# Three norms of a streaming encoder step: other homes for early split weights, four output tiles per row, and the rows' sum one chunk later

## The chip, the core and the metric

The kernel runs on one core of a Trainium2 chip. The metric is the device time of one execution in microseconds (us). Before the change it is 2686.58 us, the median of three runs (2686.34 to 2686.86). PE is TensorE's matmul stream, PEld its weight loads, DVE is VectorE, ACT ScalarE, POOL GpSimd, SP SyncE.

## What is computed

One inference step of a two-layer trunk on 288 tokens (256 of a new stream, 32 of a running one), model width 2048. Layer 0 mixes with a gated linear recurrence, layer 1 with latent attention; each is followed by a gated ConvFFN. An RMS norm stands before and after every sub-layer.

```
for layer in range(2):
    h = rms_norm(x, norm_w[layer, 0])
    m = hgrn2_mixer(h, ...) if layer == 0 else mla_mixer(h, ...)   # w_in | w_down first, w_out last
    x = x + rms_norm(m, norm_w[layer, 1])
    f, buf = conv_ffn(rms_norm(x, norm_w[layer, 2]), ...)
    x = x + rms_norm(f, norm_w[layer, 3])

def conv_ffn(h, buf, w_in, conv_w, conv_b, w_out):
    u = h @ w_in                       # 2048 -> 11264
    c = conv_b + sum(conv_w[j] * ext[:, j:j + L] for j in range(3))
    gate, up = split(c)
    return (silu(gate) * up) @ w_out   # 5632 -> 2048
```

## The kernel before

Everything is held feature-major: a row is 128 features by 288 tokens, so X has 16 rows (`KT = 16`). A matrix product is made in three fp32r matmuls, since each fp32 operand is split into a top part and the rest: h_hi with w_hi, h_lo with w_hi, h_hi with w_lo (`product`, lines 248 to 250). One product stands for these three matmuls on one row and one output tile.

Weights come in chunks: one output tile by 8 rows (128x1024, 512 KB). A chunk goes through a ring of four places (`RING`): SP loads it into `raw`, ACT writes the top part `w_hi` (`split_hi`, L235), DVE the rest `w_lo` (`split_lo`, L242), PE makes 8 products. ACT may split chunk n once PE has finished chunk n-4, whose place it takes. SP may load chunk n once DVE has split chunk n-4. One semaphore each counts splits and finished chunks, so chunks are split in number order. A GEMM is a loop of trips of four output tiles, tile t in PSUM bank t; in a usual trip tile t has chunks 2t and 2t+1. In the first trip of a GEMM behind a norm the chunks 0 to 3 are the first halves (rows 0 to 7) of the four tiles and 4 to 7 the second halves (`FIRST`).

The change is about three norms. Norm 1 stands between hgrn_out and ffn_in00, norm 2 between ffn_out01 and down (the mixer's w_down of layer 1, nine tiles), norm 3 between mla_out and ffn_in10. Each does the following:

- PE sums the squares of the previous output with a matrix of ones (L1153, L1157), and then makes 16 matmuls that nobody reads (`keep_busy`, L1167). ACT makes the root (`rstd`, L1049 and L1051).
- DVE scales the output (L1195), adds it to X (L1201), and forms h_lo (L1181), two rows at a time. ACT forms h_hi (L1108) and the squares of X (L1109). The next norm's own root is not in h: it is applied after the GEMM.
- PE starts the next GEMM on the rows as they come, the chunks 0 and 1 together: two products for each new row (`gemm_first`). Then chunks 2 to 7 follow one after the other.
- DVE adds up the 16 rows of squares (`square_sum`, L1215) and PE sums over the partitions (L316), after chunk 6. ACT makes the root RSB (`pre_stat_act`), and in the FFN then loads the table set for Silu (L1054).

In the FFN, each tile leaves its bank by ACT (`evac`, L1256), POOL scales it by RSB into `ext` (L1370, L1371) and appends old and new conv rows (L1373, L1376), DVE does the three taps (`conv`, L1325 to L1330), ACT Silu (L1260), DVE the product (`gated`, L1336), ACT and DVE split it for the next GEMM (`g_top` L1264, `g_rest` L1343). All of this stands in a fixed order in each engine's program, mixed by hand with the splits of coming weights (`ffn_act`, `ffn_dve`). `AHEAD = 3` chunks of trip 1 are split in the program of trip 0. `EARLY` says after which rows of a norm which chunk is split; `split_next` splits the next GEMM's first chunks at the end of a GEMM.

Of the kernel before, what the change touches and what calls it, by code (L numbers as in the profile page):

```python
# [23 lines left out]
P = 128  # L24
# [7 lines left out]
RING = 4  # L32
# [13 lines left out]
def trunk_program(nc, a):  # L46
# [66 lines left out]
    with ExitStack() as ctx:  # L113
# [36 lines left out]
        with ExitStack() as ffn:  # L150
            def sbf(name, shape, dt=F32):
                taken["ffn"] += 4 * math.prod(shape[1:])
                return ffn.enter_context(nc.sbuf_tensor(name, shape, dt))
            g_hi = sbf("g_hi", [P, HF, T], F32R)
            g_lo = sbf("g_lo", [P, HF, T], F32R)
            ext = sbf("ext", [P, 4, EXT])
            cv = sbf("cv", [P, 4, T + 2])
            prod = sbf("prod", [P, 2, T])
        sb("shared", [P, max(taken.values()) // 4])
# [44 lines left out]
        AHEAD = 3  # L204
        HEAD = KT // 4
        EARLY = [{}, {10: 4, 13: 5}, {10: 4, 13: 5}, {10: 4, 13: 5}]
# [48 lines left out]
        def to_split(phase, i, t):  # L255

            if isinstance(i, int) and i == 0:
                if phase in FIRST and t < 4:
                    return [6, 7] if t == 0 and phase not in ("hgrn_out", "mla_out") else []
# [29 lines left out]
        def gemm_first(pe, phase, s):  # L289
# [6 lines left out]
            for ch in (a0, a1):  # L296
                if phase == IN:

                    pe.wait_ge(lo_done, ch.number + 1)
                    for kk in range(HEAD):  # L300
                        pe.wait_ge(h_ready, kk + 1)
                        product(pe, psum[ch.tile][:, 0:T], ch, kk, H_HI[:, kk, :], H_LO[:, kk, :], kk == 0, False)
                    continue
                pe.wait_ge(evacuated, tile_number(phase, 0, ch.tile) - 3)
                pe.wait_ge(lo_done, ch.number + 1)
            for kk in range(HEAD if phase == IN else 0, a0.units):
# [664 lines left out]
        def run_out(eng, phase, split, drain, ahead=lambda: None):  # L971
# [31 lines left out]
            split_next(eng, split, phase, (0, 1, 2))  # L1003
            ahead()
            drain(eng, phase, trips - 1, n - 1)
            split_next(eng, split, phase, (3,))
# [235 lines left out]
        def ffn_act(act, layer, half, i, gemm, prev):  # L1242
# [24 lines left out]
            if stats:  # L1267

                for n in range(2):
                    split_hi(act, phase, 1, n)  # L1270
                    evac(0, n)
                pre_stat_act(act, {0: 1, 2: 3}[ffn_base(layer, half)])
                load_set(act, SILU_SET)
                split_hi(act, phase, 1, 2)
            early = half == 0 and isinstance(i, int) and i == 1
            if early:

                evac(0, 2)
                hi(1)
                evac(0, 3)  # L1280
# [10 lines left out]
            hi(2)  # L1291
# [9 lines left out]
        def ffn_dve(dve, layer, half, i, gemm, prev):  # L1301
# [43 lines left out]

            lo(0)
            if prev:
                g_rest(i - 1, 0)
                conv(i - 1, 2)
            lo(1)  # L1350
# [3 lines left out]
            lo(2)  # L1354
# [141 lines left out]
        def down_dve(dve):  # L1496
            down_splits(dve, split_lo, to_split("down", 0, 0))
            dve.memset(mx[:], 0.0)
            dve.memset(sums[:], 1.0).then_inc(filled, 1)
            square_sum(dve, 2)  # L1500
            dve.wait_ge(n_rstd, stat[2, "pre"] + 1)
            for t in range(4):
                split_lo(dve, "down", 0, 8 + t)
# [28 lines left out]
        def down_pe(pe):  # L1532
            gemm_first(pe, "down", 2)
            for k in range(8, len(CHUNKS["down"])):
                gemm_chunk(pe, "down", 0, k, H_HI, H_LO, KT)
                if k == 8:
                    pe.wait_ge(y_done, 1)
                    pe.matmul(psum[6][:, 0:T], swap[:], Y[:, 2 * LATENT, :], start=True, stop=True).then_inc(m["swapped_k"], 1)
                if k == 11:
# [356 lines left out]
        def _(dve):  # L1896
# [56 lines left out]

# [7 lines left out]
        def _(pe):  # L1961
# [7 lines left out]
            for layer in range(2):  # L1969
# [114 lines left out]
```

## Time and profile before

| | |
|---|---|
| median of three runs | 2686.58 us |
| span of the profiled execution | 2684.1 us |
| own time of the profiled execution outside its span | not shown; the median is 2.5 us over the span |
| PE busy / PEld | 99% / 98% |
| DVE / ACT / POOL busy | 66% / 49% / 15% |
| mean granted TensorE clock | 0.999 |
| DMA | 413.6 MB, 154 GB/s |

A row of a timeline gives start, duration, engine, line, operation and tiles. A matmul's duration overlaps the next one's, so that pace is read from one start to a later one. In brackets stands the idle time before the instruction and what ended it.

### The profile page before, as it was taken

How to read it: one execution, taken by the hardware profiler on the slowest of the kernel's cores; microseconds unless marked ns; L12 is line 12 of the kernel's file. 1: busy time of each engine (PE TensorE's matmuls, PEld its weight loads, DVE VectorE, ACT ScalarE, POOL GpSimd, SP SyncE). 2: the span in 40 equal slices, each digit the busy share in tenths (PEclk: the TensorE clock that was granted, in tenths of full speed). 3: DMA queues.
4: the chain of work that ended last, by engine and by line, in shares of the span. 5: the costliest groups of instructions: out<-in, count | busy, mean ns of one | idle time of the engine just before them, and what ended most of it. 6: DMA issues, size and time to landing. Idle time of an engine off the chain costs nothing.

```text
span 2684.1 us, 55341 instructions
## 1 busy us (share of the span) xinstructions
PE 2665.3 (99%) x19774; PEld 2642.2 (98%) x19774; DVE 1762.4 (66%) x2908; ACT 1303.7 (49%) x2181; POOL 405.2 (15%) x792
## 2 busy tenths in 40 slices
PE   9999999999999999999999999999999999999999
PEld 9999999999999999999999999999999999999998
DVE  7888888848776534676645865548666535666644
ACT  6565666545444333444444566545444433444443
POOL 2111111101322100222200000002322101222200
PEclk9999999999999999999999999999999999999999
DMA  6444444444545555444555422344545555545553
GB/s 239 141 140 138 143 137 132 138 168 131 176 163 165 162 165 167 164 165 163 163 166 169 141 90 90 118 157 142 172 159 169 162 165 163 170 157 168 162 165 121
DMA packets 123105, 413.60 MB, mean 154 GB/s; under 512 B 13904, under 2 KB 20208, under 8 KB 123024
## 3 DMA queue, kind: packets, MB, share of 16 engines
q1 hardware_dynamic: 114912, 406.37, 47.0%
q10 hardware_dynamic: 7056, 3.21, 0.4%
q0 software_dynamic: 1056, 2.92, 0.3%
q8 instruction: 52, 0.85, 0.1%
q14 instruction: 29, 0.24, 0.0%
HBM read 406.97 MB, written 5.48 MB: 154 GB/s over the span
## 4 chain that ended last, share of the span: by engine, by line
PE 94%; DVE 4%; ACT 1%; issue 1%; DMA 0%; DVEq 0%; ACTq 0%; SPq 0%
PE bank L248 30%; PE bank L250 29%; PE bank L249 29%; DVE w_lo L242 1%; DVE Y L1195 1%; DVE X L1201 1%; DVE h_lo L1181 1%; PE bank L1756 1%; PE bank L828 1%; DVE Y L1215 1%; PE bank L789 0%; PE bank L796 0%; PE bank L829 0%; ACT w_hi L235 0%; PE bank L1761 0%
## 5 line engine op out<-in xcount | busy, mean ns | idle before, releaser
L248 PE MATMUL bank<-h_hi,w_hi 128*128 128x288 f32 (+1 forms) x4208 | 1262.7, 300 | 10.2 <-DVE h_lo L1181 7.4
L242 DVE TENSOR_TENSOR w_lo<-raw,w_hi 128x1024 fp32r<-128x1024 f32 (+1 forms) x784 | 952.3, 1225 | 452.7 <-ACT w_hi L235 452.3
L249 PE MATMUL bank<-h_lo,w_hi 128*128 128x288 f32 (+1 forms) x4208 | 1248.9, 297 | 0.0
L250 PE MATMUL bank<-h_hi,w_lo 128*128 128x288 f32 (+1 forms) x4208 | 1245.5, 296 | 0.0
L235 ACT ACTIVATE w_hi<-raw 128x1024 fp32r<-128x1024 f32 (+1 forms) x784 | 805.9, 1037 | 848.2 <-PE bank L250 839.6
L248 PEld LDWEIGHTS bank<-h_hi,w_hi 128*128 128x128 f32 x4208 | 789.5, 188 | 16.6 <-DVE h_lo L1181 9.9
L250 PEld LDWEIGHTS bank<-h_hi,w_lo 128*128 128x128 f32 x4208 | 792.8, 188 | 0.2
L249 PEld LDWEIGHTS bank<-h_lo,w_hi 128*128 128x128 f32 x4208 | 790.9, 188 | 0.6
L1370 POOL TENSOR_TENSOR ext<-yt,small 128x256 f32<-128x256 f32 x176 | 213.2, 1211 | 1502.2 <-ACT yt L1256 1033.9
L248 PE MATMUL bank<-g_hi,w_hi 128*128 128x288 f32 x1408 | 416.8, 296 | 0.0
L249 PE MATMUL bank<-g_lo,w_hi 128*128 128x288 f32 x1408 | 415.4, 295 | 0.0
L250 PE MATMUL bank<-g_hi,w_lo 128*128 128x288 f32 x1408 | 413.9, 294 | 0.0
L250 PEld LDWEIGHTS bank<-g_hi,w_lo 128*128 128x128 f32 x1408 | 265.1, 188 | 0.0
L249 PEld LDWEIGHTS bank<-g_lo,w_hi 128*128 128x128 f32 x1408 | 264.3, 188 | 0.0
L248 PEld LDWEIGHTS bank<-g_hi,w_hi 128*128 128x128 f32 x1408 | 263.8, 187 | 0.0
L1325 DVE TENSOR_SCALAR cv<-ext,conv_w 128x290 f32<-128x290 f32 x176 | 75.9, 431 | 216.1 <-POOL conv_new L1376 216.1
L248 PE MATMUL bank<-o_hi,w_hi 128*128 128x288 f32 x496 | 147.9, 298 | 0.0
L249 PE MATMUL bank<-o_lo,w_hi 128*128 128x288 f32 x496 | 146.3, 295 | 0.0
L250 PE MATMUL bank<-o_hi,w_lo 128*128 128x288 f32 x496 | 145.8, 294 | 0.0
L1327 DVE SCALAR_TENSOR_TENSOR cv<-ext,conv_w,cv 128x290 f32<-128x290 f32 x176 | 92.7, 526 | 24.5 <-DVE cv L1325 22.3
L1330 DVE SCALAR_TENSOR_TENSOR cv<-ext,conv_w,cv 128x290 f32<-128x290 f32 x176 | 92.7, 527 | 22.5 <-DVE cv L1327 5.3
L250 PEld LDWEIGHTS bank<-o_hi,w_lo 128*128 128x128 f32 x496 | 93.4, 188 | 0.0
(266 smaller groups left out, 2102.2 us busy)
## 6 DMA issues: line engine op xcount, KB each, us to landing
raw<-in_w_fi SPq DMA_DIRECT2D x352, 512.0 KB, 4.0
raw<-in_w_hi_in SPq DMA_DIRECT2D x128, 512.0 KB, 4.0
raw<-in_w_fo SPq DMA_DIRECT2D x128, 512.0 KB, 3.5
raw<-in_w_fo SPq DMA_DIRECT2D x64, 384.0 KB, 3.4
raw<-in_w_ho SPq DMA_DIRECT2D x32, 512.0 KB, 4.1
raw<-in_w_mo SPq DMA_DIRECT2D x32, 512.0 KB, 3.9
raw<-in_w_down SPq DMA_DIRECT2D x18, 512.0 KB, 4.4
raw<-in_w_ukv SPq DMA_DIRECT2D x16, 512.0 KB, 3.7
```

Source lines behind the costliest of these rows:

```text
L235: act.activation(split_weights(ch)[0], raw[:, ch.slot, 0:ch.units * P], ACT.Copy).then_inc(hi_done, 1)
L242: dve.tensor_tensor(lo, raw[:, ch.slot, 0:ch.units * P], hi.bitcast(F32), ALU.subtract).then_inc(lo_done, 1)
L248: pe.matmul(out, top[:, w], rhs_hi, start=start, stop=False)
L249: pe.matmul(out, top[:, w], rhs_lo, start=False, stop=False)
L250: return pe.matmul(out, rest[:, w], rhs_hi, start=False, stop=stop)
L828: pe.matmul(out[:, A0:A0 + 192], key_a[:, c:c + BL], z[:, OQ:BK], start=True, stop=True)
L1181: dve.scalar_tensor_tensor(out=H_LO[:, c, :], in0=X[:, c, :], scalar=norm_w[:, lb_, wb, c:c + 1], in1=H_HI[:, c, :].bitcast(F32), op0=ALU. ...
L1195: dve.tensor_tensor(Y[:, rows, :], Y[:, rows, :], RSA.unsqueeze(1).to_broadcast([P, n, T]), ALU.mult)\
L1325: dve.tensor_scalar(cv[:, t, :], ext[:, t, 2:EXT], tap(2), tap(3), ALU.mult, ALU.add).then_inc(conv_step, 1)
L1327: dve.scalar_tensor_tensor(out=cv[:, t, :], in0=ext[:, t, 1:EXT - 1], scalar=tap(1), in1=cv[:, t, :], op0=ALU.mult, op1=ALU.add).then_inc( ...
L1330: dve.scalar_tensor_tensor(out=cv[:, t, :], in0=ext[:, t, 0:EXT - 2], scalar=tap(0), in1=cv[:, t, :], op0=ALU.mult, op1=ALU.add).then_inc( ...
L1370: pool.tensor_tensor(ext[:, t, 2:2 + TP], yt[:, t, 0:TP], RSB[:, 0:TP], ALU.mult)
```

## The change

- In the three GEMMs behind the norms (`DEEP`) the split chunks have further places. Chunk 0 goes to `lead_hi/lo`, chunks 1 to 4 to the four ring places shifted by one, chunks 5 to 7 to `rest_hi/lo`, chunks 8 and on to the ring again. The new places lie in memory that the mixers and the FFN share and that is free at that time. `raw` keeps its four places.
- `split_next` splits five chunks (0 to 4) at the end of the GEMM before, where it was four. `EARLY` splits chunks 5, 6, 7 after rows 5, 6, 8 (it was 4 and 5 after rows 10 and 13, with 6 and 7 behind the norm). `AHEAD` is 5.
- `gemm_rows` takes the place of `gemm_first` in these GEMMs: all four tiles take each row as it comes, so four products per row. The last two rows are taken tile by tile.
- The rows' sum on PE (`rows_sum`) follows the first chunk of trip 1 (chunk 8), where it followed chunk 6. On ACT the root comes after the evacuation of all four tiles; on DVE two splits stand ahead of the sum of squares.
- In trip 1 of the FFN, chunk 5 is split right at the trip's start, ahead of `g_rest(0, 0)`, and only chunks 6 and 7 come later, in `lo(3)`/`hi(3)`.
- A memset of `ext` moves behind the norm on DVE, since `ext` shares memory with `lead_lo`.

```
+    def deep_place(ch):
+        if ch.phase in DEEP and isinstance(ch.trip, int):
+            n = ch.trip * len(CHUNKS[ch.phase]) + ch.k
+            return n if n < 3 * RING else None
+        return None
...
-        AHEAD = 3
+        AHEAD = 5
...
-        EARLY = [{}, {10: 4, 13: 5}, {10: 4, 13: 5}, {10: 4, 13: 5}]
+        EARLY = [{}] + [{5: 5, 6: 6, 8: 7}] * 3
...
+            elif deep_place(ch) is not None:
+                n = deep_place(ch)
+                if n == 0 and phase == "ffn_in00":
+                    act.wait_ge(S["s_stored"], 32 * HEADS)
+                act.wait_ge(chunk_done, ch.number - (RING if n <= RING else n if n < 2 * RING else 2 * RING - 2))
...
+        def gemm_rows(pe, phase, s):
+            for kk in range(KT - 2):
+                upper = kk // UNITS
+                for t in range(4):
+                    ch = Chunk(phase, 0, 4 * upper + t)
...
+                    mm = product(pe, psum[t][:, 0:T], ch, kk - ch.start, H_HI[:, kk, :], H_LO[:, kk, :], kk == 0, False)
+                    if kk == UNITS - 1:
+                        mm.then_inc(chunk_done, 1)
+            for t in range(4):
+                ch = Chunk(phase, 0, 4 + t)
+                for kk in range(KT - 2, KT):
...
+                mm.then_inc(chunk_done, 1)
...
             if stats:
-                for n in range(2):
-                    split_hi(act, phase, 1, n)
-                    evac(0, n)
+                split_hi(act, phase, 1, 0)
+                split_hi(act, phase, 1, 1)
+                evac(0, 0)
+                evac(0, 1)
+                split_hi(act, phase, 1, 2)
+                evac(0, 2)
+                evac(0, 3)
+                split_hi(act, phase, 1, 3)
                 pre_stat_act(act, {0: 1, 2: 3}[ffn_base(layer, half)])
                 load_set(act, SILU_SET)
-                split_hi(act, phase, 1, 2)
+                split_hi(act, phase, 1, 4)
...
                     if stats and t == 0:
+                        split_lo(dve, phase, 1, 0)
+                        split_lo(dve, phase, 1, 1)
                         square_sum(dve, {0: 1, 1: 3}[layer])
-                        for n in range(AHEAD):
+                        for n in range(2, AHEAD):
                             split_lo(dve, phase, 1, n)
...
         def down_act(act):
-            down_splits(act, split_hi, to_split("down", 0, 0))
-            pre_stat_act(act, 2)
             for t in range(4):
                 split_hi(act, "down", 0, 8 + t)
                 down_out_act(act, t)
+            pre_stat_act(act, 2)
...
         def down_dve(dve):
-            down_splits(dve, split_lo, to_split("down", 0, 0))
+            down_splits(dve, split_lo, (8, 9))
             dve.memset(mx[:], 0.0)
             dve.memset(sums[:], 1.0).then_inc(filled, 1)
             square_sum(dve, 2)
+            down_splits(dve, split_lo, (10, 11))
             dve.wait_ge(n_rstd, stat[2, "pre"] + 1)
...
         def down_pe(pe):
-            gemm_first(pe, "down", 2)
+            gemm_rows(pe, "down", 2)
             for k in range(8, len(CHUNKS["down"])):
                 gemm_chunk(pe, "down", 0, k, H_HI, H_LO, KT)
                 if k == 8:
+                    rows_sum(pe, 2)
```

Three places of the programs show the moves. On PE, at the start of ffn_in00, bank n is output tile n. Before:

```order
L1167 MATMUL bank5<-ones 128x512 x16
L248 MATMUL bank0<-h_hi,w_hi 128x288
L249 MATMUL bank0<-h_lo,w_hi 128x288
L250 MATMUL bank0<-h_hi,w_lo 128x288
L248 MATMUL bank1<-h_hi,w_hi 128x288
L249 MATMUL bank1<-h_lo,w_hi 128x288
L250 MATMUL bank1<-h_hi,w_lo 128x288
L248 MATMUL bank0<-h_hi,w_hi 128x288
```

and after (`product` is at lines 277 to 279 there):

```order
L1218 MATMUL bank5<-ones 128x512 x16
L277 MATMUL bank0<-h_hi,lead_hi 128x288
L278 MATMUL bank0<-h_lo,lead_hi 128x288
L279 MATMUL bank0<-h_hi,lead_lo 128x288
L277 MATMUL bank1<-h_hi,w_hi 128x288
L278 MATMUL bank1<-h_lo,w_hi 128x288
L279 MATMUL bank1<-h_hi,w_lo 128x288
L277 MATMUL bank2<-h_hi,w_hi 128x288
L278 MATMUL bank2<-h_lo,w_hi 128x288
L279 MATMUL bank2<-h_hi,w_lo 128x288
L277 MATMUL bank3<-h_hi,w_hi 128x288
```

A row now brings four products where it brought two.

On DVE, the end of trip 0's splits and trip 1 of ffn_in00. `w_lo` is a chunk's lower split, `cv` a conv tap, `prod` the gated product, `g_lo` its split. Before:

```order
L1215 TENSOR_TENSOR ssx<-Y 128x288
L242 TENSOR_TENSOR w_lo<-raw,w_hi 128x1024 x3
L1325 TENSOR_SCALAR cv<-ext,conv_w 128x290
...
L1337 TENSOR_TENSOR prod<-cv 128x32
L242 TENSOR_TENSOR w_lo<-raw,w_hi 128x1024 x2
L1325 TENSOR_SCALAR cv<-ext,conv_w 128x290
L1327 SCALAR_TENSOR_TENSOR cv<-ext,conv_w,cv 128x290
L1330 SCALAR_TENSOR_TENSOR cv<-ext,conv_w,cv 128x290
L1343 TENSOR_TENSOR g_lo<-prod,g_hi 128x288
L242 TENSOR_TENSOR w_lo<-raw,w_hi 128x1024 x2
```

and after:

```order
L1266 TENSOR_TENSOR ssx<-Y 128x288
L271 TENSOR_TENSOR w_lo<-raw,w_hi 128x1024 x3
L1383 TENSOR_SCALAR cv<-ext,conv_w 128x290
...
L1395 TENSOR_TENSOR prod<-cv 128x32
L1383 TENSOR_SCALAR cv<-ext,conv_w 128x290
L1385 SCALAR_TENSOR_TENSOR cv<-ext,conv_w,cv 128x290
L1388 SCALAR_TENSOR_TENSOR cv<-ext,conv_w,cv 128x290
L1401 TENSOR_TENSOR g_lo<-prod,g_hi 128x288
L271 TENSOR_TENSOR w_lo<-raw,w_hi 128x1024 x2
```

The last row is, in both, chunks 6 and 7 of trip 1, behind the first conv of trip 1. The three splits under the sum are chunks 0 to 2 of trip 1 before, and 2 to 4 after.

On ACT, in `down`: `yt` is the evacuation of a tile, `small` the root. Before:

```order
L1109 ACTIVATE Y<-X 128x576
L235 ACTIVATE w_hi<-raw 128x1024 x2
L1049 ACTIVATE small<-bank,eps 128x288
L1051 ACTIVATE small<-small 128x288
L235 ACTIVATE w_hi<-raw 128x1024
L1476 ACTIVATE yt<-bank 128x288
L235 ACTIVATE w_hi<-raw 128x1024
```

and after:

```order
L1160 ACTIVATE Y<-X 128x576
L264 ACTIVATE w_hi<-raw 128x1024
L1539 ACTIVATE yt<-bank 128x288
L264 ACTIVATE w_hi<-raw 128x1024
L1539 ACTIVATE yt<-bank 128x288
```

The top split of chunk 9 now stands behind the evacuation of tile 0.

## Rows read from the trace of the kernel before

**Rows 1.** The page's chain that ended last, shares by engine.
```profile
PE 94%; DVE 4%; ACT 1%; issue 1%; DMA 0%; DVEq 0%; ACTq 0%; SPq 0%
```

**Rows 2.** Timeline of PE, norm 1 and the first trips of ffn_in00.
```profile
614.57 0.65 PE L1153 MATMUL bank<-ssq,ones 128*128 128x288 f32 x2
...
619.75 0.37 PE L248 MATMUL bank<-h_hi,w_hi 128*128 128x288 f32 x1
...
621.62 0.40 PE L248 MATMUL bank<-h_hi,w_hi 128*128 128x288 f32 x1 [0.84 <-DVE h_lo L1181]
...
646.51 0.75 PE L316 MATMUL bank<-ssx,ones 128*128 128x288 f32 x2 [0.29 <-DVE ssx L1215]
...
647.23 0.29 PE L249 MATMUL bank<-h_lo,w_hi 128*128 128x288 f32 x1
...
669.62 0.29 PE L249 MATMUL bank<-h_lo,w_hi 128*128 128x288 f32 x1
```

**Rows 3.** Timeline of DVE in norm 1.
```profile
625.40 0.94 DVE L1181 SCALAR_TENSOR_TENSOR h_lo<-X,norm_w,h_hi 128x288 fp32r<-128x288 f32 x2
...
641.22 4.74 DVE L1215 TENSOR_TENSOR Y<-Y 128x2304 f32<-128x2304 f32 x3
```

**Rows 4.** Timeline of ACT, root and first split behind it.
```profile
647.30 0.50 ACT L1049 ACTIVATE small<-bank,eps 128x288 f32<-128x288 f32 x1 [2.83 <-PE bank L316]
...
649.59 1.06 ACT L235 ACTIVATE w_hi<-raw 128x1024 fp32r<-128x1024 f32 x1
```

**Rows 5.** Timeline of DVE behind the root, ffn_in00.
```profile
651.83 0.42 DVE L1325 TENSOR_SCALAR cv<-ext,conv_w 128x290 f32<-128x290 f32 x1
...
655.38 0.43 DVE L1336 TENSOR_TENSOR prod<-cv 128x256 f32<-128x256 f32 x1
...
656.79 0.42 DVE L1325 TENSOR_SCALAR cv<-ext,conv_w 128x290 f32<-128x290 f32 x1
...
658.25 1.22 DVE L242 TENSOR_TENSOR w_lo<-raw,w_hi 128x1024 fp32r<-128x1024 f32 x1
...
661.02 0.43 DVE L1336 TENSOR_TENSOR prod<-cv 128x256 f32<-128x256 f32 x1
...
664.88 0.43 DVE L1325 TENSOR_SCALAR cv<-ext,conv_w 128x290 f32<-128x290 f32 x1 [0.51 <-POOL conv_new L1376]
...
666.90 0.45 DVE L1343 TENSOR_TENSOR g_lo<-prod,g_hi 128x288 fp32r<-128x288 f32 x1
667.26 1.21 DVE L242 TENSOR_TENSOR w_lo<-raw,w_hi 128x1024 fp32r<-128x1024 f32 x1
```

**Rows 6.** Timeline of POOL: tile 0 of trip 0, then of trip 1.
```profile
648.41 0.91 POOL L1370 TENSOR_TENSOR ext<-yt,small 128x256 f32<-128x256 f32 x1 [143.53 <-ACT small L1051]
...
649.61 0.18 POOL L1376 COPY conv_new<-ext 128x4 f32<-128x4 f32 x1
...
662.49 0.80 POOL L1370 TENSOR_TENSOR ext<-yt,small 128x256 f32<-128x256 f32 x1 [5.11 <-ACT yt L1256]
```

**Rows 7.** Busy time by stretch, norm 2 (columns: PE, PEld, DVE, ACT, POOL, PEclk, DMA, GB/s).
```profile
1475.17:1479.00 3.83, 2.09 (x12) 1.62 (x12) 3.62 (x7) 2.31 (x7) 0.00 (x0) 1.00 0.11 44
1479.00:1483.00 4.00, 4.00 (x18) 4.00 (x19) 3.79 (x7) 2.63 (x6) 0.00 (x0) 0.57 0.00 0
```

**Rows 8.** Timeline of PE and ACT, norm 2 and `down`.
```profile
1475.17 0.37 PE L248 MATMUL bank<-h_hi,w_hi 128*128 128x288 f32 x1
...
1504.57 0.39 ACT L1476 ACTIVATE yt<-bank 128x288 f32<-128x288 f32 x1
...
1509.41 0.65 PE L1538 MATMUL bank<-Y,swap 128*128 128x288 f32 x2
```

**Rows 9.** Timeline of PE, norm 3.
```profile
1819.12 0.37 PE L248 MATMUL bank<-h_hi,w_hi 128*128 128x288 f32 x1
...
1846.24 0.51 PE L316 MATMUL bank<-ssx,ones 128*128 128x288 f32 x1 [0.37 <-DVE ssx L1215]
```

More of the change, by code:

```diff
@@ L100, in __init__ @@
             self.tile, self.start, self.units = chunks_of(phase, i)[k]
+    DEEP = ("ffn_in00", "down", "ffn_in10")
+    def deep_place(ch):
[3 more added lines that the diff above has]
+        return None
     def spare_chunk(ch):
@@ L158, in trunk_program, with sbw @@
             prod = sbf("prod", [P, 2, T])
+        taken["split"] = 0
+        with ExitStack() as split:
+            def sbw(name, shape, dt=F32R):
+                taken["split"] += 4 * math.prod(shape[1:])
+                return split.enter_context(nc.sbuf_tensor(name, shape, dt))
+            sbw("below", [P, 4 * T])
+            rest_hi, rest_lo = sbw("rest_hi", [P, 3, UNITS * P]), sbw("rest_lo", [P, 3, UNITS * P])
+            sbw("between", [P, 2 * HF * T - taken["split"] // 4])
+            lead_hi, lead_lo = sbw("lead_hi", [P, UNITS * P]), sbw("lead_lo", [P, UNITS * P])
         sb("shared", [P, max(taken.values()) // 4])
@@ L258, in to_split @@
                 if phase in FIRST and t < 4:
-                    return [6, 7] if t == 0 and phase not in ("hgrn_out", "mla_out") else []
+                    return [6, 7] if t == 0 and phase == IN else []
                 return [k for k in tile_chunks(phase, i, t) if k >= 4]
@@ L296, in gemm_first @@
             for ch in (a0, a1):
[L297 to L304, printed above, removed]
                 pe.wait_ge(lo_done, ch.number + 1)
-            for kk in range(HEAD if phase == IN else 0, a0.units):
+                for kk in range(HEAD):
+                    pe.wait_ge(h_ready, kk + 1)
+                    product(pe, psum[ch.tile][:, 0:T], ch, kk, H_HI[:, kk, :], H_LO[:, kk, :], kk == 0, False)
+            for kk in range(HEAD, a0.units):
                 pe.wait_ge(h_ready, KT * s + kk + 1)
@@ L1002, in run_out @@
                 trip(1, True)
-            split_next(eng, split, phase, (0, 1, 2))
+            more = NEXT.get(phase) in DEEP
+            split_next(eng, split, phase, (0, 1, 2, 3) if more else (0, 1, 2))
             ahead()
             drain(eng, phase, trips - 1, n - 1)
-            split_next(eng, split, phase, (3,))
+            split_next(eng, split, phase, (4,) if more else (3,))
         def out_col(phase, i, t):
@@ L1290, in ffn_act @@
                 silu(i - 1, 1)
-            hi(2)
+            if not early:
+                hi(2)
             if prev:
@@ L1344, in g_rest @@
                                   ALU.subtract).then_inc(g_done, 1)
+            early = half == 0 and isinstance(i, int) and i == 1
             lo(0)
+            if early:
+                lo(1)
+                lo(2)
             if prev:
@@ L1349, in ffn_dve @@
                 conv(i - 1, 2)
-            lo(1)
+            if not early:
+                lo(1)
             if prev:
@@ L1353, in ffn_dve @@
                 gated(i - 1, 1)
-            lo(2)
+            if not early:
+                lo(2)
             if gemm:
@@ L1952, in _ @@
                     norm_dve(dve, 3)
+                    dve.wait_ge(chunk_done, Chunk("ffn_in10", 0, 0).number + 1)
                     dve.memset(ext[:, :, 0:2], 0.0)
```

42 lines of the change are left out of this document (31 added, 11 removed).

## The prediction, made before the changed kernel ran

> **What bounds the kernel now.** I read the page's chain of waits first. The reader is to see that 94% of it is PE and 4% DVE [rows 1]: the kernel is as long as its matmuls, and only what makes PE wait can be won. So I went to PE's timeline and looked for starts further apart than the pace. The pace comes from two matmuls of the same kind 56 products apart, 647.23 and 669.62 [rows 2]: 0.40 us a product, 3.2 a chunk, 25.6 for a trip of 64. PE waits at the three norms. The last product of hgrn_out is issued by 614.57, the first one of ffn_in00 starts at 619.75: 5.2 us of head that the change leaves as it is. Then each new row gives PE two products (0.8 us), but rows come 1.2 to 2 us apart: PE starts again at 621.62 after 0.84 idle, and so on [rows 2]. From 619.75 the seven chunks up to the rows' sum are 22.4 us and would end at 642.15; the sum starts at 646.51. 4.4 us are lost, 0.5 of it at the sum itself, which waits for DVE's tree of squares. The sum costs PE 0.6 on its way (646.51 to the paced start 647.23, less one matmul).
>
> **Row phase.** Nothing is removed from the work; 64 products move. With four products a row takes 1.6 us. DVE gives the rows in pairs: 4 and 5 are through at 626.34 [rows 3], a pair each 2.4 us, where PE now needs 3.2. PE will wait only for row 1 (ready for 621.62, wanted at 621.4) and row 2, some 0.25 each, with 0.1 for each restart. The three splits that now stand among the rows cost DVE 1.2 each [rows 5]; they push row 10 to 626.3 + 3 x 2.4 - 0.4 + 3 x 1.15 = 636.6, just when PE wants it, 0.2. I take 0.9 in all, bounds 0.6 and 2. Trip 0 of ffn_in00 ends at 619.75 + 25.6 + 0.9 = 646.25, chunk 8 (the first of trip 1) at 649.45 = Z, where the rows' sum now stands. With 0.6 for the sum, PE is 3.45 us ahead of the kernel before, whose trip 0 ended, by the paced start of chunk 14 at 669.5 [rows 2] less 19.2, at 650.3. Before the head there are five splits for four; the fifth stands where the fourth stood, so it costs nothing unless its load lands late (0 to 0.3).
>
> **Where the gain meets DVE.** Behind the sum all in the FFN hangs on the root. Chunks 2 to 4 of trip 1 are split without need of it or soon after, chunk 5 in time, but chunks 6 and 7 are split behind the first conv of trip 1. PE wants chunk 14 (k = 6 of trip 1) at Z + 0.6 + 16.0 = 666.05. I add up its lower split from Z: sum to root 0.79 [rows 2, 4]; root, Silu table, next top split 2.29 [rows 4]; top and lower split 2.24 [rows 4, 5]; two convs 3.55; gate 0.5; lower split of chunk 5, now ahead of them, 1.2; g_lo 0.36; two convs of 1.46; gate to POOL's start on tile 0 of trip 1 1.47 [rows 5, 6]; POOL alone 1.38, from 648.41 to 649.79 [rows 6]; conv beside POOL 2.02; g_lo 0.36; lower split of chunk 6 with its signal 1.26 [rows 5]. The sum is 20.3, so 649.45 + 20.3 = 669.8. PE waits 3.8 us for it and starts chunk 14 at 669.8, where the kernel before started it at 669.5 with its split done at 668.5. The gain of norm 1 is handed back: net 0.3 lost. The bounds: 668.6, with every conv at 1.46, and 670.8, with POOL at the 2.39 us from 662.49 to 664.88, when DVE ran beside it [rows 5, 6]. I take POOL alone, as DVE stands waiting for it in the new order. After that splits 16 and 17 come some 2 us ahead of PE, so trips 2 and on run as before. Norm 3 starts 1199.37 later [rows 9]: chunk 14 now at 1869.2, and before at 1846.24 + 22.98 = 1869.2. Net 0.
>
> The Trainium skill (SBUF — State Buffer, Who interferes with whom) says that a VectorE instruction with two SBUF inputs and a GpSimd one that reads SBUF exclude each other, and that the second one waits for the first. By that POOL's tile costs 1.38 here and not 2.39, and the sum stays; with the longer price it would be 1.0 later. The trace agrees as far as it goes: 1.38 with DVE waiting, 2.39 with a lower split beside it [rows 6, 5].
>
> **Norm 2 and `down`.** The rows give the same 0.9. First product 1475.17 [rows 8], trip 0 to 1501.7, chunk 8 to 1504.9. But here chunk 9's top split stands behind the evacuation of tile 0, and the tree of squares on DVE behind chunk 9's lower split. Tile 0 is done 6 products before the end, at 1499.3. Signal 0.2, evacuation 0.3 of its 0.39 [rows 8] until the next starts, top split 1.05, lower split 1.15, tree to PE 5.3 (641.22 to 646.51) [rows 3, 2]: 1507.3. PE waits 2.4 for the sum and is at chunk 9 at 1507.9, through it and the swap matmul (0.5) at 1511.6. Before, the swap started at 1509.41 [rows 8], and chunk 9 ended at 1509.9 + 3.2 = 1513.1. Gain 1.5; the least is 0.5, the most 3.9, if the sum is not late. Behind it the root is 3 us or more ahead of its users, and the latent roots hang on PE's own chunks, which costs nothing.
>
> **The clock.** In norm 2 the granted clock was 1.00 while PE was busy 2.09 of 3.83 us, and then 0.57 over 4 us, that is mostly the lower level, 1.2 GHz: 18 matmuls where 30 fit, 1.6 us [rows 7]. It hid in waits there. A wait of 3.8 us without one matmul is emptier than that stretch, so I expect one such fall behind each wait for chunk 14, and there no wait hides it: 2 x 1.6 = 3.2. Bounds 0 and 2 x 3.2. For the 2.4 us in `down` I take none (norms 1 and 3 had half-empty stretches without a fall). The Trainium skill (TensorE: Matmul & The Clock Gate, What's actually happening) has it that the slow level is the default and activity lifts it; rows 7 agree. It speaks against a change that gathers small waits into a large one.
>
> **The sum.** -0.3 + 0 + 1.5 - 3.2 = 2.0 us lost. The span of 2684.1 becomes 2686.1. With the 2.5 us that the median lies above the span: 2688.6.
>
> **Rivals.**
> 1. *The gain stays.* DVE's splits of chunk 6 come by 666.05: the chain would have to be 3.8 shorter than my sum of rows. Against it, every term is a row and the order is fixed in the program; for it, POOL and ACT might be free earlier than in the old trip. Then 3.45 + 3.8 + 1.5 are kept (norm 3 lost 0.35 more before): 2677.8, or 2675.4 with the sum in `down` in time.
> 2. *The waits come, the clock stays.* For it: norms 1 and 3 kept 1.00 through rows with half their time empty. 2686.6 - 1.2 = 2685.4.
> 3. *Slower.* The clock again, but for longer: down to its lower level in all three norms, and in the FFN for two stretches of rows 7 each. 5 x 1.6 - 1.2 = 6.8 lost: 2693.4. It decides from the fourth such stretch, 6.4 of clock less 1.2. For it: the waits are longer than any in the old norms; against it, dense products follow each.
>
> **Numbers.** Forecast 45%, own range 2686 to 2691.5. Rival 1 20%, rival 2 20%, rival 3 15%. A measurement of this kernel can tell 0.2%, 5.4 us, from no change: faster is under 2681.2, slower over 2692.0. Rival 1, with a remainder of partly kept gains, gives 0.22 faster; most of rival 3 and the top of the forecast 0.13 slower. The range 2677.5 to 2692 holds the forecast, rival 2 and the nearer form of rival 1; it leaves out some 8% below and 10% above.
>
> **What would show it.** After the first product of each norm, PE's starts 1.6 us apart per row with under 1 us idle in all. In ffn_in00 and ffn_in10 one wait of PE for DVE's w_lo of 2.5 to 5 us, some 20 us behind the rows' sum, and no large one elsewhere; behind it a PEclk under 1. In `down` a wait of about 2.4 us for the squares. If chunk 14 finds its split ready, or its wait is under 1 us, the step on DVE's chain is wrong, and the time is near 2678. If PE waits in rows 3 to 15, the row phase is wrong.

## The result and the profile of the changed kernel

| | before | after |
|---|---|---|
| median (least to most) of 21 runs each | 2686.55 us (2686.13 to 2686.92) | 2690.85 us (2689.88 to 2691.66) |
| span of the profiled execution | 2684.1 us | 2689.4 us |
| mean granted TensorE clock | 0.999 | 0.997 |

The ratio is 1.0016, with a 95% interval of 1.0010 to 1.0022. The changed kernel is 4.3 us slower. That is less than the 0.2% that the prediction took as the bound of a change. The forecast was 2688.6.

The page's chain answers to [rows 1]: what DVE has in it halves, and yet the kernel is slower, since a slow matmul counts as PE's own work.

```profile
PE 95%; DVE 2%; ACT 1%; issue 1%; DMA 1%; POOL 0%; ACTq 0%; SPq 0%; DVEq 0%; POOLq 0%
```

The waits of PE come next (columns: who waited for whom, us in total, times, longest).

```profile
PE bank L277 <- DVE w_lo L271: 9.2, 3, 4.2
...
PE bank L343 <- DVE ssx L1266: 2.3, 1, 2.3
```

Before, PE stood for DVE's h_lo 7.4 us in ten waits. Now there are three large waits that were not there. Two are for the lower split of chunk 14 (9.2 us with a small one), and one is for the squares in `down`. L277 to L279 are the old L248 to L250, and L343 is the old L316.

PE's timeline of norm 1 and ffn_in00 answers to [rows 2]. The last two rows stand on both sides of the wait:

```profile
620.12 0.37 PE L277 MATMUL bank<-h_hi,lead_hi 128*128 128x288 f32 x1
...
621.64 0.29 PE L279 MATMUL bank<-h_hi,w_lo 128*128 128x288 f32 x1
621.99 0.40 PE L277 MATMUL bank<-h_hi,lead_hi 128*128 128x288 f32 x1
...
636.92 0.40 PE L277 MATMUL bank<-h_hi,w_hi 128*128 128x288 f32 x1
...
649.78 0.65 PE L343 MATMUL bank<-ssx,ones 128*128 128x288 f32 x2
...
666.12 0.29 PE L279 MATMUL bank<-h_hi,w_lo 128*128 128x288 f32 x1
670.48 0.58 PE L277 MATMUL bank<-h_hi,w_hi 128*128 128x288 f32 x1 [4.07 <-DVE w_lo L271]
670.85 0.44 PE L278 MATMUL bank<-h_lo,w_hi 128*128 128x288 f32 x1
671.09 0.44 PE L279 MATMUL bank<-h_hi,w_lo 128*128 128x288 f32 x1
```

The rows now cost three restarts: for row 1 (621.99), row 2 (623.95) and row 10 (636.92). The start there comes 0.21, 0.26 and 0.15 later than the pace, and the second matmul behind it 0.11 later again, 0.9 in all. PE reaches the rows' sum 29.66 us after its first product (72 products, which at the pace are 28.8) and doesn't wait for it. In [rows 2] the sum, two chunks earlier in the program, came after 26.76. Then PE stands still from 666.12 to 670.48. Behind that the matmuls start 0.24 apart and no longer 0.13. The windows say why (columns: length, PE busy, PEclk, DMA share, GB/s):

```profile
666.30:670.48 4.18, 0.11 (x2) 0.89 0.00 2
670.48:671.50 1.02, 1.02 (x4) 0.50 0.09 12
675.50:676.50 1.00, 1.00 (x6) 0.58 0.54 156
676.50:677.50 1.00, 1.00 (x10) 1.00 0.99 242
```

In this execution the clock fell within the wait to 0.50 (1.2 GHz). It came back at about 676.4. Until then PE made six matmuls a microsecond, where ten is the usual.

DVE behind the root answers to [rows 5], POOL to [rows 6], ACT to [rows 4]:

```profile
653.85 1.23 DVE L271 TENSOR_TENSOR w_lo<-raw,w_hi 128x1024 fp32r<-128x1024 f32 x1 [2.69 <-ACT w_hi L264]
...
659.02 0.42 DVE L1394 TENSOR_TENSOR prod<-cv 128x256 f32<-128x256 f32 x1
...
664.08 0.43 DVE L1394 TENSOR_TENSOR prod<-cv 128x256 f32<-128x256 f32 x1
...
666.89 0.43 DVE L1383 TENSOR_SCALAR cv<-ext,conv_w 128x290 f32<-128x290 f32 x1 [2.29 <-POOL conv_new L1440]
...
668.70 0.50 DVE L1401 TENSOR_TENSOR g_lo<-prod,g_hi 128x288 fp32r<-128x288 f32 x1
669.12 2.35 DVE L271 TENSOR_TENSOR w_lo<-raw,w_hi 128x1024 fp32r<-128x1024 f32 x2
```
```profile
665.54 0.74 POOL L1434 TENSOR_TENSOR ext<-yt,small 128x256 f32<-128x256 f32 x1 [7.57 <-ACT yt L1307]
```
```profile
650.46 0.50 ACT L1100 ACTIVATE small<-bank,eps 128x288 f32<-128x288 f32 x1 [2.32 <-PE bank L343]
```

DVE stands 2.29 us with nothing to do, for POOL. POOL had stood 7.57 us for ACT's evacuation, which ACT's program puts behind the second top of g. Only after the conv does DVE come to chunks 6 and 7 (the x2 at 669.12).

Norm 3 repeats it, in answer to [rows 9]:

```profile
1821.25 0.37 PE L277 MATMUL bank<-h_hi,lead_hi 128*128 128x288 f32 x1
...
1871.75 0.58 PE L277 MATMUL bank<-h_hi,w_hi 128*128 128x288 f32 x1 [4.21 <-DVE w_lo L271]
```

The first products of norm 2, with windows of the same lengths as in [rows 7]: PE makes 24 matmuls where it made 12, then 30 where it made 18, and the clock doesn't fall there any more.

```profile
1478.86:1482.69 3.83, 3.68 (x24) 3.21 (x25) 3.62 (x7) 2.32 (x6) 0.00 (x0) 1.00 0.18 71
1482.69:1486.69 4.00, 4.00 (x30) 4.00 (x31) 3.90 (x7) 4.00 (x8) 0.00 (x0) 1.00 0.00 0
```

In `down`, PE and then DVE, in answer to [rows 8]:

```profile
1508.39 0.29 PE L279 MATMUL bank<-h_hi,w_lo 128*128 128x288 f32 x1
1510.96 0.75 PE L343 MATMUL bank<-ssx,ones 128*128 128x288 f32 x2 [2.28 <-DVE ssx L1266]
```
```profile
1504.51 1.23 DVE L271 TENSOR_TENSOR w_lo<-raw,w_hi 128x1024 fp32r<-128x1024 f32 x1 [3.17 <-ACT w_hi L264]
1505.68 2.55 DVE L1266 TENSOR_TENSOR Y<-Y 128x2304 f32<-128x2304 f32 x1
```

DVE stands 3.17 us for chunk 9's top part before it may begin its tree.

### The profile page after: what moved, and what is told of

It reads as the page before. It is cut to its first block, busy times and chain, and to the rows that moved or that the text cites. A ratio compares the mean times of both kernels' runs of the same rounds, so it can differ in the third digit from the quotient of the medians.

```text
span 2689.4 us, 55328 instructions
## 1 busy us (share of the span) xinstructions
PE 2667.3 (99%) x19774; PEld 2645.3 (98%) x19774; DVE 1762.1 (66%) x2908; ACT 1303.1 (48%) x2181; POOL 402.2 (15%) x792
## 3 DMA queue, kind: packets, MB, share of 16 engines
q0 software_dynamic: 1056, 2.92, 0.3%
## 4 chain that ended last, share of the span: by engine, by line
PE 95%; DVE 2%; ACT 1%; issue 1%; DMA 1%; POOL 0%; ACTq 0%; SPq 0%; DVEq 0%; POOLq 0%
PE bank L277 30%; PE bank L279 30%; PE bank L278 30%; PE bank L1821 1%; PE bank L878 1%; PE bank L839 1%; PE bank L846 0%; DVE w_lo L271 0%; DVE Y L1246 0%; PE bank L879 0%; DVE X L1252 0%; ACT w_hi L264 0%; PE bank L1826 0%; DMA raw<-in_w_fi 0%; PE bank L881 0%
## 5 line engine op out<-in xcount | busy, mean ns | idle before, releaser
L277 PE MATMUL bank<-h_hi,w_hi 128*128 128x288 f32 (+1 forms) x4112 | 1234.9, 300 | 11.6 <-DVE w_lo L271 9.2
L271 DVE TENSOR_TENSOR w_lo<-raw,w_hi 128x1024 fp32r<-128x1024 f32 (+2 forms) x772 | 936.2, 1222 | 448.4 <-ACT w_hi L264 448.0
L278 PE MATMUL bank<-h_lo,w_hi 128*128 128x288 f32 (+1 forms) x4112 | 1222.3, 297 | 0.0
L279 PE MATMUL bank<-h_hi,w_lo 128*128 128x288 f32 (+1 forms) x4112 | 1218.9, 296 | 0.0
L264 ACT ACTIVATE w_hi<-raw 128x1024 fp32r<-128x1024 f32 (+2 forms) x772 | 792.9, 1036 | 838.0 <-PE bank L279 834.2
L277 PEld LDWEIGHTS bank<-h_hi,w_hi 128*128 128x128 f32 x4112 | 772.9, 188 | 15.0 <-issue 12.7
L279 PEld LDWEIGHTS bank<-h_hi,w_lo 128*128 128x128 f32 x4112 | 776.4, 189 | 0.2
L278 PEld LDWEIGHTS bank<-h_lo,w_hi 128*128 128x128 f32 x4112 | 774.3, 188 | 0.7
L277 PE MATMUL bank<-g_hi,w_hi 128*128 128x288 f32 x1408 | 416.8, 296 | 0.0
L279 PE MATMUL bank<-g_hi,w_lo 128*128 128x288 f32 x1408 | 413.9, 294 | 0.0
L279 PEld LDWEIGHTS bank<-g_hi,w_lo 128*128 128x128 f32 x1408 | 265.2, 188 | 0.0
L277 PEld LDWEIGHTS bank<-g_hi,w_hi 128*128 128x128 f32 x1408 | 263.6, 187 | 0.0
L277 PE MATMUL bank<-o_hi,w_hi 128*128 128x288 f32 x496 | 147.9, 298 | 0.0
L279 PE MATMUL bank<-o_hi,w_lo 128*128 128x288 f32 x496 | 145.8, 294 | 0.0
L279 PEld LDWEIGHTS bank<-o_hi,w_lo 128*128 128x128 f32 x496 | 93.4, 188 | 0.0
```

Of the source, the lines that this page charges most:

```text
L271: dve.tensor_tensor(lo, raw[:, ch.slot, 0:ch.units * P], hi.bitcast(F32), ALU.subtract).then_inc(lo_done, 1)
L277: pe.matmul(out, top[:, w], rhs_hi, start=start, stop=False)
L278: pe.matmul(out, top[:, w], rhs_lo, start=False, stop=False)
L279: return pe.matmul(out, rest[:, w], rhs_hi, start=False, stop=stop)
```

## Experiments

Each ratio is against runs of the kernel before made beside that experiment. Their medians are 2686.43 to 2686.60 us in all of them, so medians of different experiments may be compared. Where starts of two traces are compared, a shift that stood before them is taken off.

**e1 and e2: is the clock behind the large waits a cost of its own?** 16 or 8 matmuls that nobody reads go into the wait for chunk 14, in both FFNs.

```
                         for k in range(8):
+                            if k == 6:
+                                keep_busy(pe, 16)      # e2: 8
                             gemm_chunk(pe, f"ffn_in{layer}0", 1, k, H_HI, H_LO, KT)
```

> The changed kernel, with 16 matmuls that nobody reads (4.1 us) on PE just ahead of chunk 14, where it waits 4.3 us for DVE in both FFNs. Theory (the clock falls because PE is empty there, and costs 2.7 us each time): chunk 14 starts when it did, the granted clock stays at 1.00, the time falls by 2 x 2.7 = 5.4 to about 2685.4. Rival (the slow matmuls behind the wait come from something else, such as weights or DMA, or the clock falls all the same): 2690.9, with the matmuls behind the wait still 0.24 us apart.

> As the one with 16 fillers, but 8 (2.0 us), so that about 2.3 us of the wait stay empty, about as much as the wait of 2.5 us in down that had no fall of the clock. Theory (only a wait emptier than that brings the clock down): no fall, 2685.4. Rival (any such wait next to this one does): the fall stays in one or both FFNs, 2688 to 2691.

Measured: e1 2687.3 us (2685.56 to 2687.54), ratio 1.0001 (0.9992 to 1.0010); e2 2689.09 (2688.46 to 2690.39), ratio 1.0011 (1.0002 to 1.0020). PE in e1:

```profile
666.18 3.81 PE L1218 MATMUL bank<-ones 128*128 128x512 f32 x16
670.43 0.37 PE L277 MATMUL bank<-h_hi,w_hi 128*128 128x288 f32 x1 [0.43 <-DVE w_lo L271]
670.64 0.29 PE L278 MATMUL bank<-h_lo,w_hi 128*128 128x288 f32 x1
```

Chunk 14 starts at the same time as without the fillers (670.43 and 670.48), so the wait is not shortened, and behind one restart the pace is 0.13. No slow matmul is left around the three norms in the profiled execution of e1 (2685.92 us), and its mean clock is 1.0. The kernel gains 3.5 us from 32 matmuls of no use: the clock is a cost of its own. The median missed the expected 2685.4 by 1.9. Four of the eleven runs had a mean clock of 1.000 and took 2685.56 to 2685.92 us; the seven others had 0.999 and took 2687.0 to 2687.54. That is one fall of the clock more, by its size. Where it lay no profile shows; the wait in `down` has no fillers.

Half as many fillers gain 1.8 us; the time is in the rival's range (2688 to 2691). They leave 2.2 to 2.4 us empty. That held the clock in ffn_in00 and lost it in ffn_in10 (14 slow matmuls from 1871.79 on) and in `down` (13). In `down` the clock fell only after PE had been busy again for more than a microsecond, from 1508.22 on (columns as in [rows 7]):

```profile
1508.22:1509.42 1.20, 1.20 (x7) 1.09 (x8) 1.20 (x2) 0.41 (x1) 0.93 (x2) 1.00 0.06 14
1509.42:1510.42 1.00, 1.00 (x7) 1.00 (x6) 1.00 (x2) 0.97 (x3) 0.66 (x2) 0.62 0.61 160
```

**e3: is it the place of chunks 6 and 7?** DVE splits both ahead of conv(1, 0), as it does chunk 5. ACT writes their top parts right behind Silu of trip 0's second half, where they stood behind the evacuation of trip 1's tile 0. The rest stays.

```
                 silu(0, 1)
+                hi(3)
...
                 evac(i, 0)
-                hi(3)
+                if not early:
+                    hi(3)
...
             if not early:
                 lo(2)
+            else:
+                lo(3)
             if gemm:
                 conv(i, 0)
...
             if gemm:
-                lo(3)
+                if not early:
+                    lo(3)
                 conv(i, 1)
```

> The changed kernel, with the splits of chunks 6 and 7 of the FFN's trip 1 moved: on ACT behind the second Silu of trip 0, on DVE ahead of the first conv of trip 1, where DVE waited 2.3 us for POOL. Theory (PE waits only because these two splits stand behind the conv that hangs on POOL): both waits of 4.3 us and both clock falls of 2.7 us go, the time is 2690.9 - 14 = about 2677. Rival (ACT and DVE are behind by their load, so that the wait only moves to chunks 15 to 18): a wait of 2 to 4 us somewhere in trip 2, 2683 to 2689.

Measured: 2680.46 us (2679.35 to 2680.82), ratio 0.9976 (0.9966 to 0.9986). The two waits of 4.3 us are gone and so are the falls behind them: 10.4 us less than the changed kernel. It missed the expected time by 3.5 us, for two reasons that the trace shows. First, a smaller wait appeared one trip later, once in each FFN:

```profile
673.48 0.40 PE L277 MATMUL bank<-h_hi,w_hi 128*128 128x288 f32 x1 [0.91 <-DVE w_lo L271]
```

Against the pace it is 1.08 here and 1.12 in ffn_in10. DVE's row for the conv of trip 1's tile 0 tells where it comes from:

```profile
667.83 0.89 DVE L1385 TENSOR_SCALAR cv<-ext,conv_w 128x290 f32<-128x290 f32 x1 [1.21 <-POOL conv_new L1445]
```

DVE waits there for POOL. POOL's product on that tile lay beside DVE's two splits, and took 1.79 us where it took 0.74 in the changed kernel:

```profile
665.42 1.79 POOL L1439 TENSOR_TENSOR ext<-yt,small 128x256 f32<-128x256 f32 x1 [7.70 <-ACT yt L1307]
```

Second, the wait in `down` now had a fall of the clock behind it, 13 slow matmuls from 1506.53 to 1509.41. This fall is not in every run: three of the nine had a mean clock of 1.000 and took 2679.35 to 2679.56 us.

**e4: is it the late sum?** The sum goes right behind trip 0, with one split ahead of DVE's tree where there were two.

```
                         gemm_rows(pe, f"ffn_in{layer}0", 2 * layer + 1)
+                        rows_sum(pe, 2 * layer + 1)
                         for k in range(8):
                             gemm_chunk(pe, f"ffn_in{layer}0", 1, k, H_HI, H_LO, KT)
-                            if k == 0:
-                                rows_sum(pe, 2 * layer + 1)
```

> The changed kernel, with the FFN's rows' sum on PE right behind trip 0 instead of behind chunk 8, and the tree of squares on DVE behind one split instead of two. Theory (all up to chunk 14's split is a chain of 20.3 to 20.7 us from the sum): PE waits about 1 us for the sum, the root comes some 2 us earlier, the wait for chunk 14 shrinks from 4.3 to 1 to 2.5 us, and the clock does not fall: 2690.9 - 2 x (2 + 2.7) = about 2681. Rival (the place of the sum does not matter, DVE's load sets chunk 14): the wait stays near 4 us and the time within 1 us of 2691.

Measured: 2687.36 us (2687.04 to 2688.76), ratio 1.0004 (0.9995 to 1.0013).

```profile
647.77 0.75 PE L343 MATMUL bank<-ssx,ones 128*128 128x288 f32 x2 [1.07 <-DVE ssx L1266]
```
```profile
669.71 0.37 PE L277 MATMUL bank<-h_hi,w_hi 128*128 128x288 f32 x1 [2.00 <-DVE w_lo L271]
```

The wait for chunk 14 shrinks to 2.17 against the pace, and a wait of 1.23 for the sum comes in. Together they are 0.8 to 1.0 shorter than the one wait was. In the profiled execution, the slowest of the eleven, the clock still fell in all three norms, for 13 or 14 matmuls each time; eight of the runs were 1.0 to 1.7 us faster than it, with a mean clock of 0.999 where it had 0.998. So halving a wait did not always remove the fall behind it. The gain is 3.5 us, where 10 was expected and under 1 by the rival. The trace shows a reason on ACT. The root starts 1.9 us earlier (648.56, was 650.46), but the next top split, that of chunk 12 (k = 4 of trip 1), then has to wait for PE to free its place in the ring:

```profile
651.80 1.06 ACT L264 ACTIVATE w_hi<-raw 128x1024 fp32r<-128x1024 f32 x1 [0.96 <-PE bank L279]
```

DVE's first conv starts only 0.9 earlier for it (654.07, was 654.99). The chain to chunk 14 did not hang on the sum alone. The place of the sum is a minor part beside that of chunks 6 and 7.

**e5: the wait in `down`.**

```
         def down_act(act):
+            split_hi(act, "down", 0, 8)
             for t in range(4):
-                split_hi(act, "down", 0, 8 + t)
+                if t < 3:
+                    split_hi(act, "down", 0, 9 + t)
                 down_out_act(act, t)
```

> The changed kernel with one edit in `down` alone: ACT writes the top part of chunk 9 ahead of the evacuation of tile 0, as it does for chunk 8. My theory: the 2.44 us for which PE waits there for DVE's tree of squares come from that evacuation, which makes chunk 9's lower split, and the tree behind it, late. Without it the wait shrinks by about 2.2 us, and nothing in that norm gives it back, since the latent roots hang on PE's own chunks: 2690.9 - 2.2 = 2688.7 us. The two waits of 4.3 us and the clock falls behind them stay as they are. Rival: the tree is late for another reason (its own length on DVE), the wait stays over 1.5 us, and the time is above 2690.

Measured: 2687.83 us (2686.19 to 2688.88), ratio 1.0004 (0.9995 to 1.0013). DVE in `down`:

```profile
1499.30 2.36 DVE L271 TENSOR_TENSOR w_lo<-raw,w_hi 128x1024 fp32r<-128x1024 f32 x2 [0.84 <-ACT w_hi L264]
1501.61 2.55 DVE L1266 TENSOR_TENSOR Y<-Y 128x2304 f32<-128x2304 f32 x1
```

Chunks 8 and 9 are now split in one go, the tree follows without its stop, and PE doesn't wait for the sum at all (0.21 of restart stays). The gain is 3.0 us, 0.8 over the 2.2 expected. A fall of the clock behind that wait, which the first profile of the changed kernel didn't show and e9 and e10 do, is the likely rest.

**e6 and e7: the parts together.** e6 is e3 with e5. e7 adds one line:

```
                 g_top(0, 0)
+                evac(1, 0)
                 silu(0, 1)
                 hi(3)
...
             if gemm and not stats:
-                evac(i, 0)
+                if not early:
+                    evac(i, 0)
```

> The kernel of e3 (chunks 6 and 7 of trip 1 split ahead of the convs that wait for the root; 2680.5 us) together with the edit of e5 in `down`. Its trace had one fall of the clock left, behind the 2.4 us wait in `down`, with 13 matmuls at the slow pace (1.4 us). Theory: wait and fall go together, 2.2 + 1.4, so 2676.9 us; the two waits of 1.1 us at the start of trip 2 stay. Rival A: the two edits don't add up, because the fall moves to the next gap (the clock stays low somewhere for as long): 2678.3. Rival B: nothing but noise under 1 us: 2680.

> e6 with one edit more: in trip 1 of the FFN, ACT evacuates tile 0 of that trip ahead of Silu of the second half, instead of behind the splits of chunks 6 and 7 and the second top of g. In e3 POOL could start on that tile only at about 665.6, DVE stood 1.21 us for it, and everything behind it, with the split of trip 2's first chunk, was late: PE waited 1.1 us at the start of trip 2 in both FFNs. Theory: POOL starts some 5 us earlier, DVE doesn't wait, the 1.1 us waits shrink below 0.3: 2 x 0.9 = 1.8 less than e6, about 2675. Rival: POOL's tile now lies beside DVE's convs and makes them longer by about as much as the wait was (a conv's first tap has 0.85 instead of 0.42 beside POOL): no change against e6, the 1.1 us waits stay.

Measured: e6 2676.92 us (2676.82 to 2677.31), ratio 0.9964 (0.9951 to 0.9978); e7 2675.61 (2675.28 to 2676.13), ratio 0.9960 (0.9946 to 0.9973). In e6 the edits add up to what was expected, and the mean clock is 1.0. In e7 POOL starts on trip 1's tile 0 at 660.30, and DVE goes from its pair of splits to the conv without a stop:

```profile
664.88 2.35 DVE L271 TENSOR_TENSOR w_lo<-raw,w_hi 128x1024 fp32r<-128x1024 f32 x2
667.15 0.86 DVE L1387 TENSOR_SCALAR cv<-ext,conv_w 128x290 f32<-128x290 f32 x1
```

```profile
660.30 0.80 POOL L1441 TENSOR_TENSOR ext<-yt,small 128x256 f32<-128x256 f32 x1 [2.51 <-ACT yt L1307]
```

The 1.1 us waits are gone. Part of the gain goes back: a g_lo beside POOL took 0.99 where it had 0.45 in e3, and chunk 14 is late by 0.17 and 0.32. e7 is 1.3 faster than e6, where 1.8 was expected. It is the fastest kernel here, 11.0 us faster than before and 15.2 faster than the change.

**e8: what the four-tile rows are worth.** On e3, `gemm_rows` takes chunks 0 and 1 together row by row and then chunks 2 to 7 one after the other. Splits and the sum stay.

```
-            for kk in range(KT - 2):
-                upper = kk // UNITS
-                for t in range(4):
-                    ch = Chunk(phase, 0, 4 * upper + t)
...
+            for kk in range(a0.units):
+                pe.wait_ge(h_ready, KT * s + kk + 1)
+                for ch in (a0, a1):
...
+            for k in range(2, 8):
+                gemm_chunk(pe, phase, 0, k, H_HI, H_LO, KT, (h_ready, KT * s) if k == 4 else None)
```

> The kernel of e3 with the rows taken again by two tiles at a time behind the three norms (chunks 0 and 1 together, then 2 to 7 one after the other), all splits and the late sum left as they are. It prices the four-tile rows. Theory: the two-tile rows lose 4.4 - 0.9 = 3.5 us in each norm. In norms 1 and 3 all behind hangs on PE's own sum, so it is kept whole; in norm 2 it takes the place of the 2.4 us wait for the squares, and costs 1.1, and the clock's fall behind that wait (1.4 us) may go: 2680.5 + 3.5 + 1.1 + 3.5 - (0 to 1.4) = 2687.2 to 2688.6 us. Rival: the rows come from DVE, which is as fast as before, so that PE gains nothing from four tiles that it doesn't wait for later: within 1.5 us of 2680.5.

Measured: 2691.79 us (2691.34 to 2693.66), ratio 1.0021 (1.0012 to 1.0031), 11.3 over e3. The expected cost was 6.7 to 8.1. The waits of PE:

```profile
PE bank L277 <- DVE h_lo L1224: 13.3, 15, 1.7
```

Against the pace PE loses 1.01, 1.06, 0.70, 1.83 and 0.67 at the starts of five rows of norm 1. With the second matmuls behind them, the rows' sum stands 34.60 us behind the first product, where it stands 29.66 in e3: 5.8 lost and 0.9. The 1.83 ends behind DVE's row of a split among the rows:

```profile
626.23 1.22 DVE L271 TENSOR_TENSOR rest_lo<-raw,rest_hi 128x1024 fp32r<-128x1024 f32 x1
```

So the row order is worth 4.9 a norm with these splits. The expected 3.5 compares with the old kernel, where no split stood among the first eight rows. Three times 4.9, less the 2.44 of the wait in `down` and its fall (1.5), both gone here, is 10.8; the medians give 11.3, the two spans 10.5. With two-tile rows and all the rest of the change, moved splits included, the kernel is 5.2 us slower than before.

**e9 and e10: the clock once more, in the unedited changed kernel.**

> The changed kernel once more, nothing edited, for a second profile of the clock. Behind waits of about the same 4.3 us one profile of it had 23 matmuls at the slow pace in each FFN, and the kernel of e5 14 and 19. Theory A: how long the clock stays low behind a wait isn't set by the wait; it differs from execution to execution, and this profile has other counts (anything from 13 to 25) behind the same two waits, and may have a fall in `down`. Theory B: it is set by the kernel's own order, and the counts are 23 and 23 again, with none in `down`.

> The changed kernel a third time, nothing edited. Theory A (it differs from execution to execution): counts of slow matmuls unlike those of the other two profiles. Theory B (set by the kernel): 23 and 23, none in `down`.

Measured, one run each: 2690.12 and 2689.82 us. The table has the matmuls that start 0.24 apart, counted in each timeline. In brackets stands what the fall cost in us, by starts: the way from the end of the wait to the first product of the next norm (to the end of the span for the last), less the same way where the clock did not fall (e1 for the FFNs, the first profile for `down`).

| | behind 4.2 in ffn_in00 | behind 2.4 in `down` | behind 4.3 in ffn_in10 | together |
|---|---|---|---|---|
| first profile | 23 (2.6) | 0 | 23 (2.7) | 46 (5.3) |
| e9 | 10 (1.3) | 8 (1.5) | 11 (1.4) | 29 (4.2) |
| e10 | 14 (1.5) | 14 (1.5) | 13 (1.5) | 41 (4.5) |
| e5 (no wait in `down`) | 14 (1.5) | - | 19 (2.3) | 33 (3.8) |

A matmul of a product costs 0.107 more at the low level. In e9's `down` the fall took in the rows' sum itself, whose second matmul starts 0.64 behind its first and not 0.35, so that a count of 8 costs as much as one of 14. The waits are the same in all of them; the fall is not. Two of e9's stretches, behind the wait in ffn_in00:

```profile
672.00:673.00 1.00, 1.00 (x6) 0.50 0.85 279
673.00:674.00 1.00, 1.00 (x8) 0.73 0.89 307
674.00:675.00 1.00, 1.00 (x10) 1.00 0.79 311
```

Theory A holds, with two counts (10 and 11) under the 13 that it gave as the least. The two groups of runs in e1 say the same of one kernel without a second profile.

## Why the prediction was right, and which term was off

The mechanism was right: the gain of the rows is made, and handed back in one wait for chunk 14. The size was not: 4.3 us are lost by the medians, where 2.0 were forecast. The range held it because the bounds of the clock's term were wide. Starts in the two traces give the sum, as after less before:

| term | forecast, lost | measured, lost | from |
|---|---|---|---|
| before norm 1 | 0 | 0.4 | first product 620.12, was 619.75 |
| norm 1 without the clock | 0.3 | 0.6 | chunk 14 at 670.48, was 669.5 |
| clock in ffn_in00 | 1.6 | 2.7 | norm 2's first sum of squares 3.69 later (1473.17, was 1469.48), less 1.0 |
| norm 2 and `down` | -1.5 | -1.55 | shift 3.69 before it, 2.14 at norm 3 (1816.08, was 1813.94) |
| norm 3 without the clock | 0 | 0.4 | chunk 14 2.5 later (1871.75, was 1869.2) |
| clock in ffn_in10 | 1.6 | 2.8 | shift 5.3 at the end, less 2.5 |
| together | 2.0 | 5.3 | spans 2689.4 and 2684.1 |

By the medians the loss is 4.3; the profiled execution had the most slow matmuls of three.

- *Row phase.* Forecast 0.9 lost per norm; measured 0.9, at the rows that were named (1, 2 and 10). The sum stands 29.66 behind the first product, forecast 29.70 (649.45 less 619.75).
- *DVE's chain.* Forecast 20.3 from the sum to chunk 14's split; measured 20.7 (649.78 to 670.48). Most of the difference is in the two pairs of convs: 4.03 (654.99 to 659.02) where the sum had 3.55, and 3.11 (660.97 to 664.08) where it had 2.92. Two terms came out as taken. From the second gate to POOL's start are 1.46 (forecast 1.47), and from POOL's start to DVE's conv 1.35 (forecast 1.38). POOL alone was the right price: its product took 0.74 here. The row that the price was taken from, 648.41, has 0.91, and a split of DVE still lay beside its first 0.3. The wait was 4.2, forecast 3.8.
- *e3 bears the cause out.* With only chunks 6 and 7 moved the wait is gone. Rival 1, the gain that stays, stood at 2677.8. e3 reached 2680.5 with the waits at trip 2 (2.2) and one fall (1.4) still in it; less these it is 2676.9.
- *`down`.* Wait 2.4, gain 1.5: both as forecast, in the profiled execution. In e9 and e10 a fall of the clock behind the wait costs 1.5 and takes the gain back. e5 shows chunk 9's top part, behind the evacuation, as the cause.
- *The clock: the term that was mis-sized.* The step "so I expect one such fall behind each wait for chunk 14" was right about the place. Its size, 1.6 us, is that of the fall of the kernel before [rows 7]. That fall was over within the stretch: 14 matmuls 0.24 apart, from 1479.39 to 1482.75, and then the pace is back.

```profile
1482.00:1483.00 1.00, 1.00 (x6) 1.00 (x6) 0.90 (x2) 0.48 (x1) 0.00 (x0) 0.62 0.00 0
1483.00:1484.00 1.00, 1.00 (x9) 0.97 (x8) 1.00 (x3) 0.67 (x2) 0.00 (x0) 1.00 0.00 0
```

A fall has no one size. In the profiled execution the clock stayed low for 23 counted matmuls each time, 2.6 to 2.8 us; in e9 and e10 for 10 to 14, 1.3 to 1.5 us, but with a third fall of 1.5 us in `down`, where I had taken none. An execution paid 4.2 to 5.3 us to the clock, where the sum had 3.2. That is inside my bounds of 0 to 6.4. What sets the length of a fall stays open. e1 confirms rival 2's price: its four runs at a mean clock of 1.000 took 2685.56 to 2685.92, against the 2685.4 that the rival gave.
- *The 0.4 ahead of norm 1* is not shown to come from the change; no experiment looked at it. In the changed kernel the first product of the whole run starts at 8.73, in e10, which has the same code, at 8.42, and before at 8.31. Norm 1's first product starts at 620.12, at 620.26 in e9 and at 619.57 in e10, so it varies by 0.7 with nothing edited; before it was 619.75.

Rival 3, slower for longer falls in all three norms, was nearer to the truth than I gave it: three falls are what e9 and e10 show. It missed in its size: it gave 8.0 to the clock, and 6.8 lost.

## What to carry to other kernels

When a tensor engine is given work earlier, follow the next user of each thing that was not moved: here a weight split stood behind a conv, the conv behind another engine's tile, and the whole gain waited there. Moving two splits on ACT and two on DVE ahead of that chain, in each FFN, turned a loss of 4.3 us into a gain of 6.0 (e3); two moves more on ACT, in `down` and for one evacuation, made it 11.0 (e7). Price a wait on TensorE with what the clock costs behind it. Read that from the starts after the wait, up to the point where the pace is back, and in more than one execution. If an unavoidable wait is long, matmuls of no use in it can be the cheaper way.

## What the runs showed of the hardware

- A wait without matmuls costs more than itself. Behind 4.2 to 4.4 us of it the clock fell to 0.50 in all eight cases seen (four profiles, two waits each). Behind 2.2 to 2.5 us it fell in some executions and not in others: for `down`, five falls in seven profiles (no fall in the first profile of the changed kernel and in e1). Behind 1.1 us there was none in e3 and e6. But two waits of 1.0 and 1.1 us close together, in norm 2 of the kernel before, had one behind them [rows 7].
- How long it stays low is not told by the wait: 10 to 23 matmuls, 1.3 to 2.7 us of cost, behind the same 4.2 us.
- The fall need not come within the wait. In e10 the clock was at 0.94 over the first 1.09 us behind the wait in ffn_in00 and at 0.50 after that; in e2's `down` it was at 1.00 for 1.20 us behind the wait and at 0.62 in the next microsecond.
- POOL's product on trip 1's tile 0 took 0.74 us with DVE idle (changed kernel, 665.54) and 1.79 beside DVE's two splits (e3, 665.42).
